# Values stationary in two column halves and probabilities divided before the turn, in the attentions of a fused two-block kernel

## What is computed

```
# layers 0 and 3: window of 128 keys, 4 key heads for 16 query heads,
# a sink logit per head joins the denominator
s = einsum(q, k) * 64**-0.5 ; s = where(ok, s, NEG) ; m = max(s.max(-1), sink)
p = exp(s - m) ; l = p.sum(-1) + exp(sink - m)
o = einsum(p, v) / l
h = o.reshape(B, S, 1024) @ w_o + b_o

# layer 2: with 256 tokens there is one block, so this is plain causal attention
o = softmax(causal(q @ k.T * 64**-0.5)) @ v ; h = o @ w_o
```

## Time and profile before

| | us |
|---|---|
| time, median of 3 runs | 2354.15 (2353.82 to 2355.65) |
| the profiled execution | 2353.8 |
| its span, first to last instruction | 2352.0 |
| TensorE busy | 2308.6 |
| VectorE busy | 1453.5 |
| ScalarE busy | 1305.4 |
| GpSimd busy | 330.6 |

### The profile page before, as it was taken

One profiled execution on the slowest core, in us unless ns is written; L12 is line 12 of the kernel. 1 busy time (PEld: TensorE's weight loads), 2 busy tenths in 40 slices (PEclk: granted clock), 3 DMA queues, 4 the chain that ended last, 5 costly groups with the idle time before them and its releaser, 6 DMA issues.

```text
span 2352.0 us, 36560 instructions
## 1 busy us (share of the span) xinstructions
PE 2308.6 (98%) x15272; PEld 2067.4 (88%) x15272; DVE 1453.5 (62%) x2217; ACT 1305.4 (56%) x1958; POOL 330.6 (14%) x307
## 2 busy tenths in 40 slices
PE   7999999999999999999999999999999999999999
PEld 5799978888899888998789989899899898998998
DVE  6655555546645546546764567575677686765875
ACT  5554465555544556445564467565665675655654
POOL 0100032212100313001010002343000013530000
PEclk9999999999999999999999999999999999999999
DMA  6255443333455534555345544444455453444553
GB/s 266 90 212 183 179 178 138 141 134 126 179 190 187 197 141 157 196 182 203 113 173 186 194 178 148 144 162 162 179 187 189 175 184 126 162 164 160 201 193 126
DMA packets 58180, 398.92 MB, mean 170 GB/s; under 512 B 6816, under 2 KB 7072, under 8 KB 11680
## 3 DMA queue, kind: packets, MB, share of 16 engines
q1 hardware_dynamic: 56864, 393.75, 46.7%
q10 hardware_dynamic: 1152, 2.83, 0.3%
HBM read 395.51 MB, written 1.05 MB: 169 GB/s over the span
## 4 chain that ended last, share of the span: by engine, by line
PE 82%; DVE 9%; ACT 6%; POOL 2%; issue 1%; DMA 0%; SPq 0%; ACTq 0%; DVEq 0%; POOLq 0%
PE b L1280 12%; PE b L1282 12%; PE b L1281 12%; PE b L1178 12%; PE b L1179 12%; PE b L1180 12%; PE b L1183 5%; DVE wlo L1931 4%; PE b L1187 4%; ACT whi L1581 2%; ACT b L1577 1%; DVE xb L2229 1%; PE b L1246 1%; PE b L1247 1%; ACT S L1578 1%
## 5 line engine op out<-in xcount | busy, mean ns | idle before, releaser
L1931 DVE TENSOR_TENSOR wlo<-raw,whi 128x2048 fp32r<-128x2048 f32 x362 | 845.1, 2339 | 446.4 <-ACT whi L1581 446.1
L1581 ACT ACTIVATE whi<-raw 128x2048 fp32r<-128x2048 f32 x362 | 690.5, 1913 | 426.2 <-PE b L1282 221.9
L1280 PE MATMUL b<-xh,whi 128*128 128x256 f32 x2560 | 723.9, 283 | 1.0 <-DVE wlo L1931 0.7
L1282 PE MATMUL b<-xh,wlo 128*128 128x256 f32 x2560 | 712.4, 278 | 0.0
L1281 PE MATMUL b<-xl,whi 128*128 128x256 f32 x2560 | 711.6, 278 | 0.0
L1280 PEld LDWEIGHTS b<-xh,whi 128*128 128x128 f32 x2560 | 480.3, 188 | 5.6 <-DVE wlo L1931 3.3
L1281 PEld LDWEIGHTS b<-xl,whi 128*128 128x128 f32 x2560 | 481.4, 188 | 1.9
L1282 PEld LDWEIGHTS b<-xh,wlo 128*128 128x128 f32 x2560 | 481.1, 188 | 0.0
L1178 PE MATMUL b<-whi,xh 128*128 128x512 f32 x640 | 262.9, 411 | 1.5 <-DVE wlo L1931 1.5
L1178 PE MATMUL b<-whi,oh 128*128 128x512 f32 x656 | 259.0, 395 | 0.6 <-DVE ol L2220 0.6
L1179 PE MATMUL b<-wlo,oh 128*128 128x512 f32 x656 | 256.1, 390 | 0.0
(11 more groups left out here) (238 smaller groups left out, 2904.2 us busy)
## 6 DMA issues: line engine op xcount, KB each, us to landing
raw<-in_w SPq DMA_DIRECT2D x362, 1024.0 KB, 4.8
gt<-in_rows SPq DMA_DIRECT2D x8, 512.0 KB, 4.0
bt<-in_rows SPq DMA_DIRECT2D x8, 512.0 KB, 4.9
abq<-in_rows ACTq DMA_DIRECT2D x2, 768.0 KB, 6.3
x<-in_x SPq DMA_DIRECT2D x1, 1024.0 KB, 6.6
bc<-in_rows SPq DMA_DIRECT2D x4, 256.0 KB, 5.0
out<-x SPq DMA_DIRECT2D x4, 256.0 KB, 2.0
msk<-in_masks SPq DMA_DIRECT2D x1, 768.0 KB, 21.3
```

What stands on the lines that cost most here:

```text
L1280: pe.matmul(out, wh[:, k, cs], ah[:, kk, :], start=kk == 0 and s == 0, stop=False, skip_group_check=True)
L1282: last = pe.matmul(out, wl[:, k, cs], ah[:, kk, :], start=False, stop=final and k == 3, skip_group_check=True)
L1581: return ac.activation(out, i, ACT.Copy)
L1931: ve.tensor_tensor(B.wlo[r][:, :], B.raw[r][:, :], B.whi[s][:, :], ALU.subtract).then_inc(sem["loV"], 1)
```

## The change

In kinds a and c the lag between the scores of a pair and its turn grows from one visit to two (`LAG`), and that of its values from two to three; the loop has one visit more. The turn moves ahead of values and scores in the visit. A new step `share` divides the probabilities of pair v-1 by l in S itself, ahead of the turn: head 0 on VectorE, head 1 on GpSimd, two multiplications each; it is put at the end of visit v. In `pv` v is now stationary, 64 columns, and the turned probabilities stream 128 columns; head 0 writes the output partitions 0 to 63 and head 1 those from 64 to 127, so the outputs come out with head channels on partitions, and no turn of `og` is needed. A new step `opair` after `exp` copies them out of PSUM (VectorE, two copies of 128 columns), copies them to `oh` (ScalarE) and subtracts for `ol` (GpSimd). `heads` is gone, and `opart` for these mixers. The first use of a block of rows waits for `olo` of its second pair. Every second pair's turned probabilities go to `og[2]` in place of `PT`.

```diff
@@ -521,8 +521,8 @@
-        due = []
-        for v in range(n + 2):
+        due, lag = [], LAG[KIND[a]]
+        for v in range(n + lag + 1):
             if v % 4 == 0 and v < n:
...
@@ -530,40 +530,44 @@
                 tail(due.pop(0)[0])
+            turned = lag <= v < n + lag
             for i in range(2):
                 self.bank(("S", a, v, i), SB[i])
-                if 1 <= v <= n and (dv == 64 or i == 0):
+                if turned and (dv == 64 or i == 0):
                     self.bank(("T", a, v, i), TB[i if dv == 64 else v % 2])
-            if v >= 2:
-                self.step("pv", a, v - 2, dv, n)
+                    b, m = self.use["T", a, v, i]
+                    self.copied[a, v - lag, i] = (f"empty{b}", m + 1)
+            if turned and lag == 2:
+                self.step("probs", a, v - 2)
+            if v > lag:
+                self.step("pv", a, v - lag - 1, dv, n)
             if v < n:
...
                 for i in range(2):
-                    if v < 2:
+                    if v <= lag:
                         self.scored[a, v, i] = (f"empty{SB[i]}", self.use["S", a, v, i][1] + 1)
...
                     self.counts("exp", (a, v, i))
-            if v >= 2 and sinks is not None:
-                consume(v - 2)
-            if 1 <= v <= n:
-                for i in range(2 if dv == 64 else 1):
-                    b, m = self.use["T", a, v, i]
-                    self.copied[a, v - 1, i] = (f"empty{b}", m + 1)
+            if turned and lag == 1:
                 self.step("probs", a, v - 1)
...
                 weigh(v)
-            if v >= 2:
-                if sinks is None:
-                    consume(v - 2)
+            if v > lag:
+                consume(v - lag - 1)
                 if v % 2 and tail is not None:
                     due.append(((v - 2) // 2, v))
+            if lag == 2 and 1 <= v <= n:
+                self.counts("sums", (a, v - 1))
+                self.counts("shared_v", (a, v - 1))
+                self.counts("shared_g", (a, v - 1))
+                self.step("share", a, v - 1)
             for t in range(pace):
...
@@ -571,6 +575,12 @@
             tail(g)
+
+    def out_pair(self, i, pair, a, v):
+
+        self.counts("ohi", (i, "pair", pair))
+        self.counts("olo", (i, pair))
+        self.step("opair", i, pair, a, v)
...
@@ -649,13 +659,11 @@
             def consume(v):
-                self.step("heads", u0, v, v // 4)
-
-            def tail(g):
-                self.out_part((i, g), g // 2)
-                ready[g] = True
+                self.out_pair(i, v, u0, v)
+                if v % 2:
+                    ready[v // 2] = True
             self.side.append(self.attention(u0, 8, "ma", lambda u: ("q", u) in turned, consume,
-                                            lambda v, k: 2 * (v // 4) + (2 * (v % 4) + k) // 4, 64, 16 * j, tail))
+                                            lambda v, k: 2 * (v // 4) + (2 * (v % 4) + k) // 4, 64, 16 * j))
         self.project("a_w_o", j, i, ready, self.boundary, 6)
...
@@ -680,7 +688,9 @@
                         if i == 2:
-                            self.step("heads", u, gr, hh)
+                            self.out_pair(i, 4 * hh + gr, u, gr)
+                            if gr % 2:
+                                ready[2 * hh + gr // 2] = True
                         else:
...
@@ -695,10 +705,10 @@
                     def tail(gr):
-                        self.out_part((i, 2 * hh + gr), hh if i == 2 else 0)
+                        self.out_part((i, 2 * hh + gr), 0)
                         ready[2 * hh + gr] = True
                     yield from self.attention(u, 4, "mc" if i == 2 else f"mb{g}", lambda u: True, consume,
-                                              lambda v, k: v, 64, None, tail if i == 2 or g == 2 else None,
+                                              lambda v, k: v, 64, None, tail if g == 2 else None,
                                               before=u - 1 if g else None,
...
@@ -1126,6 +1136,7 @@
 KIND = "aabbbbbbccaadd"
+LAG = {"a": 2, "b": 1, "c": 2, "d": 1}
...
@@ -1288,8 +1299,11 @@
         if src == "o":
-            b, n = use["opart", a // 2, blk]
-            p.wait_ge(f"empty{b}", n + 1)
+            if a // 2 in (0, 2, 3):
+                p.wait_ge("olo", mark["olo", (a // 2, 2 * blk + 1)])
+            else:
+                b, n = use["opart", a // 2, blk]
+                p.wait_ge(f"empty{b}", n + 1)
         elif src[0] == "h":
...
@@ -1368,10 +1382,13 @@
         for i in range(1 if joined else 2):
-            b, n = use["T", a, v_ + 1, i]
+            b, n = use["T", a, v_ + LAG[KIND[a]], i]
             S = B.S[2 * (v_ % 2) + i]
...
                 p.wait_ge("joined", mark["joined", (a, v_)])
+            elif KIND[a] in "ac":
+                name = ("shared_v", "shared_g")[i]
+                p.wait_ge(name, mark[name, (a, v_)])
             else:
...
@@ -1399,11 +1416,25 @@
             return
+        if KIND[a] in "ac":
+            for t in range(2):
+                b, n = use["S", a, v_ + 3, t]
+                p.wait_ge(*o.copied[a, v_, t])
+                p.wait_ge(f"empty{b}", n)
+            for t, k, at in ((0, 0, 0), (1, 0, 128), (1, 1, 256)):
+                b = use["S", a, v_ + 3, t][0]
+                for i in range(2):
+                    c = 64 * (v_ // 2) if KIND[a] == "a" else 128 * p_ + 64 * i
+                    last = mm(B.bank[b][64 * i:64 * i + 64, 384:512], v[:, k, c:c + 64], B.turned(a, v_, i)[:, at:at + 128],
+                              k == 0, k == t)
+                if k == t and v_ + 3 >= pairs:
+                    last.then_inc(sem[f"full{b}"], 1)
+            return
         for i in range(2):
...
             p.wait_ge(f"empty{b}", n)
-            c = 64 * (v_ // 2) if KIND[a] == "a" else 128 * p_ + 64 * i
+            c = 128 * p_ + 64 * i
             pt, out = B.PT[i], B.bank[b][:, 384:512]
...
@@ -1705,14 +1733,20 @@
     def probs(first, v):
-        b, n = use["T", first, v + 1, 0]
+        b, n = use["T", first, v + LAG[KIND[first]], 0]
         a.wait_ge(f"full{b}", n + 1)
-        copy(B.PT[0][:, 0:384], B.bank[b][:, 0:384]).then_inc(sem[o.copied[first, v, 0][0]], 1)
+        copy(B.turned(first, v, 0)[:, 0:384], B.bank[b][:, 0:384]).then_inc(sem[o.copied[first, v, 0][0]], 1)
...
         act(e, e, ACT.Exp).then_inc(sem["stat_a"], 1)
+
+    def opair(i, pair, first, v):
+        for t in range(2):
+            b, n = use["S", first, v + 3, t]
+            a.wait_ge(f"empty{b}", n + 1)
+        copy(B.oh[:, pair, :], B.opair(pair)).then_inc(sem["ohi"], 1)
...
@@ -2131,9 +2165,9 @@
             return
-        b, n = use["T", a, pair + 1, 1]
+        b, n = use["T", a, pair + LAG[KIND[a]], 1]
         v.wait_ge(f"full{b}", n + 1)
-        ve.tensor_copy(B.PT[1][:, 0:384], B.bank[b][:, 0:384]).then_inc(sem[o.copied[a, pair, 1][0]], 1)
+        ve.tensor_copy(B.turned(a, pair, 1)[:, 0:384], B.bank[b][:, 0:384]).then_inc(sem[o.copied[a, pair, 1][0]], 1)
...
@@ -2141,18 +2175,25 @@
-    def heads(a, pair, hh):
+    def share(a, pair):
         u, p = o.pair(a, pair)
...
         v.wait_ge("exp", mark["exp", (a, pair, 1)])
-        i = v.mine(ve.reciprocal(B.rl[:, s, 0:4], B.l[u % 4][:, 4 * p:4 * p + 4]))
-        values(a, pair, 1)
-        v.wait_ge("own_v", i)
-        for i in range(2):
-            c = 128 * p + 64 * i
-            src, gone = values(a, pair, i)
-            r = B.rl[:, s, 2 * i:2 * i + 2].unsqueeze(2).broadcast_to([128, 2, 64])
-            ve.tensor_tensor(B.og[hh][:, :, c:c + 64], src, r, ALU.mult).then_inc(sem[gone], 1)
+        if pair >= 2:
+            v.wait_ge("shared_g", mark["shared_g", (a, pair - 2)])
+        ve.reciprocal(B.rl[:, s, 0:4], B.l[u % 4][:, 4 * p:4 * p + 4]).then_inc(sem["sums"], 1)
+        v.wait_ge("sums", mark["sums", (a, pair)])
+        S = B.S[2 * (pair % 2)]
+        for t, cs in enumerate((slice(0, 128), slice(129, 385))):
+            last = ve.tensor_scalar(S[:, cs], S[:, cs], B.rl[:, s, t:t + 1], None, ALU.mult)
+        last.then_inc(sem["shared_v"], 1)
+
+    def opair(i, pair, a, v_):
+        for t in range(2):
+            b, n = use["S", a, v_ + 3, t]
+            v.wait_ge(f"full{b}", n + 1)
+            ve.tensor_copy(B.opair(pair)[:, 128 * t:128 * t + 128],
+                           B.bank[b][:, 384:512]).then_inc(sem[f"empty{b}"], 1)
...
@@ -2533,6 +2574,17 @@
+    def share(a, pair):
+        s, S = pair % 2, B.S[2 * (pair % 2) + 1]
+        g.wait_ge("sums", mark["sums", (a, pair)])
+        for t, cs in enumerate((slice(0, 128), slice(129, 385))):
+            last = ge.tensor_scalar(S[:, cs], S[:, cs], B.rl[:, s, 2 + t:3 + t], None, ALU.mult)
+        last.then_inc(sem["shared_g"], 1)
+
+    def opair(i, pair, a, v):
+        g.wait_ge("ohi", mark["ohi", (i, "pair", pair)])
+        ge.tensor_tensor(B.ol[:, pair, :], B.opair(pair), B.oh[:, pair, :], ALU.subtract).then_inc(sem["olo"], 1)
+
```

(19 more changed lines are left out.)

## The result

The changed kernel takes 2415.95 us (median of four runs, 2412.15 to 2421.39) against 2354.32 us for the kernel before: a ratio of 1.0263, with an interval of 1.0251 to 1.0276. It is 61.6 us slower, where 31 were forecast; the time lies above the range. The profiled execution is the longest of the four, 2421.39 us with a span of 2419.6, so the traces differ by 67.6 us.

What follows compares the result with a forecast made beforehand. TensorE, busy 98% of the span, was taken as the bound, with new waits for GpSimd's share outweighing its shorter queue: 2353.8 + 20.6 (sink mixers) + 3.7 (third mixer) + 7 (clock) = 2385 us, 1.3% slower; range 2362 to 2403 us.

Steps and rivals of the forecast that it cites:

- GpSimd's share at 1.1 us: GpSimd's two multiplications of S (128 and 256 columns) per pair: 1.1 us together, the low end of 1.1 to 2.6.
- the clock at 7 us: Granted clock low after some of nine waits of 3.5 us or more: 0 to 13.5 us, half taken, 7 us.
- Queues: Order in a visit: GpSimd's share of v-1 stands behind ol, which waits for oh behind exp(v); chain 6.0 us.
- 3 to 4 us foretold: TensorE idle ahead of the turning for GpSimd's share, three or four times 3 to 4 us in each sink mixer.
- TensorE's own work: Per pair, values 0.85 us instead of 1.37, column halves side by side; og transposes gone, 5.2 us.
- Rival (b): Values steps: column halves run one after another, 0.65 us longer each, +11 us, 2396 us; chance 0.13.
- 17.7 us: Work taken off TensorE's queue: 12.5 us from the values and 5.2 us from the og transposes.
- Rival (c): GpSimd slower than its best row: share 2 us, not 1.1, in some 13 places, +12 us, 2397 us; chance 0.12.
- a gain of 3.2 us and 1.2 us of waiting for the first share: Sink mixer unit 0 until visit 4: 3.2 us saved, 1.2 us waited; scores(4) at about 66.35, not 68.37.
- Cycle of 7.5 us: Sink mixers from visit 5 on: scores follow each other about 7.5 us apart; before, 5.7, 5.5 and 4.4 us.
- Row wait, 3.9 us: Sink mixers: the output projection's first row step waits 3.9 us for oh and ol of pair 1, behind exp(4).
- Third mixer: Unit 8 net 0; unit 9, beside the output projection, loses 3.7 us through waits of 3.6 and 1.5 us.

Runs made afterwards that it cites:

- One exchange of steps: Changed kernel with the step share put before the out-pair in the visit, nothing else moved: 2376.3 us, ratio 1.0092.
- best version: Changed kernel with out-pair before the exponentials, share of v-1 in the next visit behind the turning, sink mixers' row steps one visit later: 2350.4 us; repeated, 2351.4 us.
- filled kernel: Changed kernel with overwritten dummy passes where TensorE waits: 20 in 13 places, 34 before each sink mixer's first row step: 2397.4 us.

## Why the prediction was right or wrong

The sign and the mechanism were right, the size was half of the real one. Two terms of the sum were mis-sized: GpSimd's share at 1.1 us, and the clock at 7 us.

**Queues.** Right. The share of v-1 waits for the out-pair's oh behind exp(v). One exchange of steps takes back 40 us. The single waits came out shorter than the 3 to 4 us foretold: TensorE waits for GpSimd five times in unit 0 and four times in unit 10, 1.9 to 3.7 us each, and only one in each is over 3 us; up to 1.0 us of waiting for VectorE's half stands ahead of them.

**TensorE's own work.** Right: 0.81 us for the values at full clock, 0.85 predicted, and no og transposes. Rival (b) fell. The Trainium skill's sentence on distinct column groups (TensorE: Matmul & The Clock Gate, "Why this matters for your kernels") agrees with the trace: the passes to the two halves start 5 to 7 ns apart. These savings exist, but at most a fraction of the 17.7 us reached the span: the third mixers gain 4.3 us in the best version, the sink mixers end near where they were. There the saving went into waits, it seems, since fewer microseconds of TensorE's work lie between two visits: in the best version TensorE still idles 0.75 us ahead of the turning at 80.47 for a copy of ScalarE (PT), which stands behind the conversion of a weight.

**GpSimd's share, 1.1 us.** Mis-sized. Alone it is 0.61 + 0.93 = 1.54 us, and the ol subtraction 0.73 and not 0.61. I had rows of 1.49 to 3.42 us for one form of 512 columns and scaled the lowest by columns. But 128 columns take 0.60 us and 256 take 0.92, which is by estimate 0.28 us for each instruction and 0.32 for each 128 columns; that gives 1.56 us for the old row, and the share has the fixed part twice. I also set the long rows aside, "since the long ones ran beside VectorE's weight subtraction, which has its own slots between visits". The second half of that sentence was wrong: the share released late falls just into those slots, and there it takes 3.6 to 3.9 us. Rival (c) named the cause but priced it at 12 us. From the rows its price would be 21 us by estimate: 0.44 + 0.11 us alone in some 13 places are 7 us; five long shares at 1.95 us and three long subtractions with a share behind them (100.94, 877.78, 1226.74) at 1.5 us are 14 us. The filled kernel shows that to be too high. At full clock its loss is 43.0 us, or 38.3 without the 4.7 us of filling, where the forecast without the clock had 24.3: so about 14 us are left for GpSimd and for all else that the timelines had wrong. The share also spoiled the early visits, where I had a gain of 3.2 us and 1.2 us of waiting for the first share: at 56.04 the turning waits 2.44 us for a share of 3.58 us. Scores(4), which I had at 66.35, start at 75.41, and at 68.15 even in the best version.

**Cycle of 7.5 us.** Right where GpSimd was alone (7.56 us in the filled kernel), too short beside a wlo (9.06) or at the low clock (8.59 from 87.61 to 96.20, and 10.82 to the next, with a wlo besides).

**Row wait, 3.9 us.** Right: 3.91 us at 80.98, put down to issue, with the row step behind it. Released one visit later, it goes at no cost.

**Third mixer.** Predicted 0 and 3.7 us for units 8 and 9; measured +4.7 and +7.0, for the two reasons told: long shares at 869.68 and 922.29, and low clock at 881 and 932.

**The clock, 7 us.** Mis-sized, and this is the larger error: at least 18.6 us by the filled kernel, about 23 by the estimate there. I counted nine places of one visit each and took half. The rows show stretches of 6.8 us and more behind waits that are shorter than those I counted (2.44 us at 56.04 lies beside the first one, which begins at 55.1), and a stretch takes not only the 2.3 us of turning, values and scores but the streamed steps too: two row steps behind 80.98 last 5.08 us, 2.82 at full clock.

The 30.6 us by which the forecast was short are thus, as reckoned here, some 14 us at full clock and some 16 of clock. The split rests on one run and on an estimate of its overrun. How much of the 14 us is GpSimd's own speed, how much its standing still beside wlo, and how much other errors of the timelines is argued, not shown by a run: no run takes the wlo away. That 51 us hang on GpSimd's part in the share, place and speed together, is shown by the kernel with all slices on VectorE.

## What to carry to other kernels

Ask of each step that is moved what it stands behind on each in-order queue, and put the operation that others wait for ahead of the one that itself waits; here one exchange was worth 40 us, and where it stood first on VectorE it held up others in turn. Work for GpSimd on the path must be priced beside the two-input SBUF instructions of VectorE that will run then, at its own time plus what is left of theirs; here that was up to 2.3 us on an instruction of 0.93. A change that adds waits to TensorE can pay for them twice: here waits of 2 to 4 us came with eleven stretches of 6.8 us or more at half clock, and such a stretch must be charged for all that TensorE has to do in it.

## What the runs showed of the hardware

- GpSimd nearly stands still while a VectorE subtraction of two SBUF operands runs that began first: 0.93 us became 2.86 with 2.07 us of overlap, 0.72 became 2.24 with 1.65. The forecast had this only in rival (c).
- When GpSimd began first, VectorE lost much less than the overlap. At 1197.00 a wlo that began 0.24 us behind a GpSimd slice lasted 2.48 us in place of 2.28, that slice 1.03 in place of 0.93, and the GpSimd copy of 128x4 that came next 1.79 in place of 0.19. In the kernel with the share ahead of the out-pair three wlo that began 0.19 us behind a slice lasted 2.42 us, beside slices of 0.92. The slice at 69.85 is the exception.
- The Trainium skill's "roughly line-rate" for one-input work on GpSimd (GPSIMD Engine Reference, "4.1 Engine selection") is not borne out by this form: 0.60 us for 128 columns and 0.92 for 256, where VectorE takes 1.01 us for all four slices, 768 columns.
- Two 64-column halves of the array run side by side for fp32 passes: six pairs in 0.81 us, and with one half issued wholly ahead of the other 1.05, where the one-after-the-other estimate was 1.4.
